# Moving the norm between two transformer blocks behind the first weights of the second block

## What is computed

```
def first_block(x, ...):
    h = x
    for l in range(DEPTH):
        ...
        h = h + 0.5 * swiglu_ffn(rms_norm(h, ffn2_norm[l]), ffn2_w_in[l], ffn2_w_out[l])
    return rms_norm(h, final_norm)

def second_block(x, ...):
    for l in range(DEPTH):
        x = x + 0.5 * swiglu(rmsnorm(x, norm_ffn1[l]), w_ffn1_in[l], w_ffn1_out[l])
        ...
    return rmsnorm(x, norm_final)
```

## Time and profile before

| | us |
|---|---|
| median of 3 runs | 2809.01 |
| lowest and highest | 2804.11, 2813.02 |
| the profiled execution: its own time | 2811.83 |
| its span from first to last instruction | 2809.9 |
| PE busy | 2701.6 (96% of the span) |
| DVE busy | 1546.6 (55%) |
| ACT busy | 1381.6 (49%) |
| POOL busy | 236.2 (8%) |

### The profile page before, as it was taken

One profiled execution on the slowest core, in us unless ns is written; L12 is line 12 of the kernel. 1 busy time (PEld: TensorE's weight loads), 2 busy tenths in 40 slices (PEclk: granted clock), 3 DMA queues, 4 the chain that ended last, 5 costly groups with the idle time before them and its releaser, 6 DMA issues.

```text
span 2809.9 us, 39469 instructions
## 1 busy us (share of the span) xinstructions
PE 2701.6 (96%) x14978; PEld 2312.9 (82%) x14978; DVE 1546.6 (55%) x2107; ACT 1381.6 (49%) x2168; POOL 236.2 (8%) x147
## 2 busy tenths in 40 slices
PE   8999899899999998989999999999999999999998
PEld 6879887788888898877887889888888888888887
DVE  5556735455555566455555556456555554556654
ACT  5447235454544452445544444455544444455543
POOL 0100201000000002100010000342000000243000
PEclk9999999999999999999999999999999999999999
DMA  6554213355555441244854554324555555323553
GB/s 246 187 172 155 69 48 118 111 176 186 180 187 187 136 142 39 83 129 129 220 188 159 184 187 155 109 98 150 180 187 181 186 187 166 120 94 125 195 186 136
DMA packets 117659, 426.48 MB, mean 152 GB/s; under 512 B 12988, under 2 KB 14780, under 8 KB 117116
## 3 DMA queue, kind: packets, MB, share of 16 engines
q1 hardware_dynamic: 117008, 423.55, 45.8%
q10 hardware_dynamic: 492, 0.68, 0.1%
HBM read 422.74 MB, written 1.44 MB: 151 GB/s over the span
## 4 chain that ended last, share of the span: by engine, by line
PE 89%; DVE 6%; ACT 3%; issue 1%; DMA 0%; POOL 0%; DVEq 0%; ACTq 0%
PE bank L433 73%; PE bank L453 3%; PE bank L1446 2%; DVE lo_slots L421 2%; PE bank L625 1%; PE bank L1493 1%; PE bank L1462 1%; ACT hi_slots L407 1%; PE bank L572 1%; PE bank L990 1%; PE bank L1001 0%; PE bank L782 0%; PE bank L771 0%; ACT xn L540 0%; PE bank L1476 0%
## 5 line engine op out<-in xcount | busy, mean ns | idle before, releaser
L421 DVE TENSOR_TENSOR lo_slots<-raw,hi_slots 128x1024 fp32r<-128x1024 f32 x740 | 914.8, 1241 | 797.0 <-ACT hi_slots L407 796.9
L407 ACT ACTIVATE hi_slots<-raw 128x1024 fp32r<-128x1024 f32 x788 | 830.8, 1057 | 690.7 <-PE bank L433 663.3
L433 PE MATMUL bank<-hi_slots,x_hi 128*128 128x512 f32 x1600 | 635.1, 397 | 14.3 <-DVE x_lo L604 8.9
L433 PE MATMUL bank<-hi_slots,x_lo 128*128 128x512 f32 x1600 | 625.4, 391 | 0.0
L433 PE MATMUL bank<-lo_slots,x_hi 128*128 128x512 f32 x1600 | 624.3, 390 | 0.0
L433 PE MATMUL bank<-x_hi,hi_slots 128*128 128x256 f32 x1280 | 376.3, 294 | 3.3 <-DVE x_lo L604 2.3
L433 PE MATMUL bank<-x_lo,hi_slots 128*128 128x256 f32 x1280 | 367.3, 287 | 0.0
L433 PE MATMUL bank<-x_hi,lo_slots 128*128 128x256 f32 x1280 | 366.6, 286 | 0.0
L433 PEld LDWEIGHTS bank<-hi_slots,x_hi 128*128 128x128 f32 x1600 | 301.9, 189 | 77.0 <-issue 13.2
L433 PEld LDWEIGHTS bank<-hi_slots,x_lo 128*128 128x128 f32 x1600 | 301.4, 188 | 64.3
L433 PEld LDWEIGHTS bank<-lo_slots,x_hi 128*128 128x128 f32 x1600 | 302.1, 189 | 59.5
(11 more groups left out here) (294 smaller groups left out, 2967.0 us busy)
## 6 DMA issues: line engine op xcount, KB each, us to landing
raw<-w_full SPq DMA_DIRECT2D x792, 512.0 KB, 3.3
bias_mem<-bias_rows SPq DMA_DIRECT2D x8, 288.0 KB, 6.9
const<-consts SPq DMA_DIRECT2D x1, 1664.0 KB, 7.1
h<-x_t SPq DMA_DIRECT2D x1, 1024.0 KB, 5.1
mem<-mem_t SPq DMA_DIRECT2D x1, 1024.0 KB, 10.2
final<-finals SPq DMA_DIRECT2D x2, 512.0 KB, 7.4
out_t<-h SPq DMA_DIRECT2D x4, 256.0 KB, 2.3
bias_rows<-final ACTq DMA_DIRECT2D x1, 384.0 KB
```

Source lines behind the costliest of these rows:

```text
L407: nc.scalar.activation(w_hi[s], raw[s][:, :], ACT.Copy).then_inc(hi_ready[s], 1)
L421: nc.vector.tensor_tensor(w_lo[s], raw[s][:, :], w_hi[s].bitcast(F32), ALU.subtract).then_inc(lo_ready[s], 1)
L433: mm = nc.tensor.matmul(out, lhsT=a, rhs=b, start=start and n == 0, stop=stop and n == len(passes) - 1)
```

## The change

The change gives the block seam the form of a layer seam. The first half of the unscaled `h` is transposed in the middle of the last down units and the second half after the first unit of the second block. The gain that goes with `x_hi` and `x_lo` is the product `seam_gain` of the first block's final gain and the second block's first gain, computed once at the program's start. The factor per token of the first norm is kept in `rstd_first`. `h` is still rescaled in place, now while PE works on the first up group; then the second norm's squares, mean, roots and reciprocals follow, and `rstd` becomes the product of both factors, which the first `Silu` waits for (`rstd_both`). These steps are placed between the first three splits of the new FFN. The parameters grow by 8 columns, from 440 to 448.

```diff
+        def dve_seam_state(E):
+            state = E.state(0)
+            dve.wait_ge(sems["rstd"], state * TT)
+            nc.vector.tensor_copy(rstd_first[:, :], rstd[:, :]).then_inc(sems["rstd_first"], 1)
+            dve.wait_ge(sems["final_loaded"], 16)
+            for hf in range(2):
+                two = slice(hf * HALF, (hf + 1) * HALF)
+                for t in range(TT):
+                    nc.vector.scalar_tensor_tensor(out=h[:, t, two], in0=h[:, t, two], scalar=rstd[:, t:t + 1],
+                                                   in1=final[:, two], op0=ALU.mult, op1=ALU.mult).then_inc(sems["h_ready"], 1)
+        def dve_seam_mean(E):
+            dve.wait_ge(sems["rstd_first"], 1)
+            dve_mean(E.state(0))
+        def dve_seam_rstd(E):
+            state = E.state(0)
+            for t in range(TT):
+                dve_rstd(state, t)
+            dve.wait_ge(sems["rstd"], (state + 1) * TT)
+            nc.vector.tensor_tensor(rstd[:, :], rstd[:, :], rstd_first[:, :], ALU.mult).then_inc(sems["rstd_both"], 1)
+            dve.wait_ge(sems["rstd_both"], 1)
...
+        def act_ffn(E, u0, n, state, late, opening=()):
             f = E.ffn(n)
             for i in range(3):
                 split_hi(E, u0 + i)
+                if i < len(opening):
+                    opening[i](E)
+            if opening:
+                act.wait_ge(sems["rstd_both"], 1)
...
-                    pe_ffn(E, 0, E.normed(0), 0, turn(E.state(0), 1, FFN_TURNS), nothing)
+                    pe_ffn(E, 0, E.normed(0), 0, turn(E.state(0) - seam, 1, FFN_TURNS), nothing)
...
-                    late = turn(E.state(n_last), 0, FFN_TURNS) if E.l < DEPTH - 1 else nothing
+                    late = turn(E.state(n_last), 0, FFN_TURNS) if E.block == 0 or E.l < DEPTH - 1 else nothing
...
+                    nc.vector.tensor_tensor(seam_gain[:, :], param[:, AT_FINAL:AT_REL],
+                                            param[:, AT_SECOND + SECOND_COLS["ffn1"][0]:AT_SECOND + SECOND_COLS["ffn1"][1]],
+                                            ALU.mult).then_inc(sems["seam_gain"], 1)
...
+                        now = gain(after, "ffn1", 0, KT) if E.l < DEPTH - 1 else seam_gain
...
                         dve_turned(normed, 1, FFN_TURNS, now)
                         for t in range(TT):
                             dve_rstd(state, t)
+                        if E.l == DEPTH - 1:
+                            E.block, E.l = 1, 0
+                            dve_seam_state(E)
+                            E.block, E.l = 0, DEPTH - 1
```

More of the change, by code:

```diff
@@ L255, in build @@
         rstd = sb("rstd", [P, TT])
+        rstd_first = sb("rstd_first", [P, TT])
+        seam_gain = sb("seam_gain", [P, KT])
         ffn_mem, mix1, cross, mix2 = ExitStack(), ExitStack(), ExitStack(), ExitStack()
@@ L1992, in _ @@
                 first = E.state(0)
-                act_turned(E.normed(0), 0, FFN_TURNS, gain(E, "ffn1", 0, KT))
                 if E.block == 0:
+                    act_turned(E.normed(0), 0, FFN_TURNS, gain(E, "ffn1", 0, KT))
                     for s in range(2):
                         first_hi(s)
[L1997 to L2000, removed]
+                    act_turned(E.normed(0), 1, FFN_TURNS, gain(E, "ffn1", 0, KT))
+                    for s in range(2, SLOTS):
+                        first_hi(s)
+                    for hf in range(2):
+                        for t in range(TT):
+                            act_square(first, hf, t)
                     for t in range(TT):
-                        act_square(first, hf, t)
-                for t in range(TT):
-                    act_root(first, t)
+                        act_root(first, t)
                 for E.l in range(DEPTH):
@@ L2008, in _ @@
                         nc.scalar.activation(ab_now_hi[:, :], p1(E, "ab", 0, KT * 8), ACT.Copy).then_inc(sems["ab_hi"], 1)
-                    act.wait_ge(sems["rstd"], (E.state(0) + 1) * TT)
-                    act_ffn(E, 0, 0, E.state(1), nothing)
+                    if E.block == 0 or E.l > 0:
+                        act.wait_ge(sems["rstd"], (E.state(0) + 1) * TT)
+                    act_ffn(E, 0, 0, E.state(1), nothing, (act_seam_squares, act_seam_root) if E.block == 1 and E.l == 0 else ())
                     act_full(E.state(1), E.normed(1), FFN_TURNS, gain(E, "mix", 0, KT))
@@ L2044, in _ @@
                         after.block, after.l = E.block, E.l + 1
-                        now = gain(after, "ffn1", 0, KT)
+                        now = gain(after, "ffn1", 0, KT) if E.l < DEPTH - 1 else seam_gain
+                        if E.l == DEPTH - 1:
+                            act.wait_ge(sems["seam_gain"], 1)
                         act_ffn(E, E.last(), 1, state, lambda: act_turned(normed, 0, FFN_TURNS, now))
@@ L2075, in _ @@
                 gain = (p1, p2)[E.block]
[L2076 to L2084, removed]
+                if E.block == 0:
+                    dve_turned(E.normed(0), 0, FFN_TURNS, gain(E, "ffn1", 0, KT))
+                    for s in range(2):
+                        first_lo(s)
+                    dve_turned(E.normed(0), 1, FFN_TURNS, gain(E, "ffn1", 0, KT))
+                    for s in range(2, SLOTS):
+                        first_lo(s)
+                    dve_mean(E.state(0))
+                    for t in range(TT):
+                        dve_rstd(E.state(0), t)
+                    nc.vector.tensor_tensor(seam_gain[:, :], param[:, AT_FINAL:AT_REL],
+                                            param[:, AT_SECOND + SECOND_COLS["ffn1"][0]:AT_SECOND + SECOND_COLS["ffn1"][1]],
+                                            ALU.mult).then_inc(sems["seam_gain"], 1)
                 for E.l in range(DEPTH):
@@ L2090, in _ @@
                                                 ALU.subtract).then_inc(sems["ab_lo"], 1)
-                    dve_ffn(E, 0, 0, 1, nothing)
+                    dve_ffn(E, 0, 0, 1, nothing, (dve_seam_mean, dve_seam_rstd) if E.block == 1 and E.l == 0 else ())
                     if E.block == 0 and E.l == 0:
```

26 lines of the change are left out of this document (19 added, 7 removed).

## The result

| | before | after |
|---|---|---|
| median, us | 2806.99 (5 runs) | 2791.10 (5 runs) |
| lowest and highest | 2802.35, 2813.02 | 2788.39, 2793.49 |
| the profiled execution: its own time, its span | 2811.83, 2809.9 | 2793.49, 2791.5 |

The ratio is 0.9943, 95% interval 0.9928 to 0.9958. The kernel gained 16 us, where 8.9 were forecast. The time lies 2 us under the range.

A forecast was written before the change was run, and what follows sets the result against it. PE, busy 96% of the span, was taken as the bound, with time to win only where it idles or clocks lower. Gain 9.20 - 0.3 - 0 = 8.9 us, from 2809.01 to 2800.1 us, range 2793 to 2808.

The forecast's parts named there:

- The seam: Block seam: its stretch becomes a layer seam's plus a small wait of PE; net gain 8.9 us.
- Gross 9.20: Block seam's 55.90 us less a layer seam's 46.70, from first half's addition to first hidden transposes.
- a stall of 0.3: PE waits 0.3 us for the first product `hid` after group 1's first unit; bounds 0 and 0.7.
- The stretch: From the first half's addition to the first hidden transposes at the block seam: 47.0 us, within 46.7 to 47.4.
- The chain behind it: Second norm's work on DVE and ACT beside the first up group; `hid` ready at 2170.9, PE wants it at 2170.62.
- The slot 0 remainder: On DVE at the block seam, ends some 10.5 us after the last down matmul's start, 1.6 us early for PE.
- the Trainium skill's figure: Table load ahead of the first Silu: a further drain of about 1.38 us; stall 1.7 us, gain 7.5 us.
- What else is added: `seam_gain` at the start is hidden; the parameters' load grows by 8 columns, counted 0, at most 0.1 us.
- More than 9.2: Rival: a larger gain, needing another place that the seam disturbs now; chance 0.04.
- Slower: Rival: late rescalings on DVE hold back unit 4 and all splits; 0.3% slower at 19 us late; chance 0.02.
- given back later: Rival: weights' stream is the real limit, PE waits later instead; time 2806 to 2809 us; chance 0.05.
- the bound of 0.3%: Whole kernel: least change told from none, 8.4 us, so faster means below 2800.6 us; chance of faster 0.51.

The follow-up runs named there:

- 32 bytes more: The changed kernel with an unused tile of 32 bytes per partition behind its new tiles; 2797.37 us, ratio 0.9963.
- the run with 32 bytes of padding ahead of `x_hi`: The kernel before with 32 unused bytes ahead of `x_hi` and 32 behind `x_lo`; 2828.64 us, ratio 1.0071.
- before + 32: The kernel before with one unused tile of 32 bytes per partition ahead of the FFN's tiles; 2807.62 us, ratio 0.9998.
- before + 64: The kernel before with an unused tile of 64 bytes per partition ahead of the FFN's tiles; 2806.69 us, ratio 0.9989.
- the last version: The changed kernel with 64 bytes of padding and the mixers' copy of `x` 192 bytes further on; 2779.04 us, ratio 0.9890.

## Why the prediction was wrong, step by step

**The seam: right.** Gross 9.20 less a stall of 0.3 was 8.9; it was 9.1. The stretch was forecast at 47.0 and is 46.07. Of the difference 0.71 is the faster down pitch, which isn't the seam's; 0.15 is the stall, which was 0.15 us instead of 0.3 (PE started on `hid` 0.38 us after the last matmul, where 0.23 is the pitch). With 32 bytes more, at the old pitch, the stretch is 46.68.

**The chain behind it: right within 0.3 us.** The slot 0 remainder ends at 1504.07 + 1.23 = 1505.30, 10.3 us after the last down matmul's start (forecast 10.5). The copy took 0.17 (I took 0.12). The first Silu starts 1.30 us after its table load, as in the earlier trace rows. By the Trainium skill's figure ("ScalarE: Activation LUTs", section "What ACT_TABLE_LOAD costs") another 1.38 us would lie there; this trace shows none of it either. The clock is 1.00, the eight early transposes are there, and no wait for `lo_slots` at group 1.

**"What else is added": the failed step.** The prediction costed the new tiles by the instructions that fill them and said "I count 0, at most 0.1". What they did was push `hid_hi` and `hid_lo` by 96 bytes, from distance 96 to 192 of the slots, and so take 5 ns off each of 2112 down matmuls. By the stretches that is a term of -10.7 us for the down phases; the up groups' +1.7 comes with it. Sum with both: 9.1 + 10.7 - 1.7 = 18.1 for 8.9, by the two profiles; by the medians it is 15.9. The rival that held it was "More than 9.2", which "would need another place that the seam disturbs now, for which I see no row", with a chance of 0.04. There was no row of before that could give its size; but the addresses of both programs could have been compared, and that all the FFN's buffers shift was to be seen there. The right use would have been a wider range, to both sides: the run with 32 bytes of padding ahead of `x_hi` shows that a shift can as well cost 20 us.

**The range.** That the time fell out of it has a share of chance. The forecast stands 9.0 us above the measured time; 7.0 are the gain that it lacked, and 2.0 are the median of before, which came out at 2806.99 with five runs where the prediction started from 2809.01 with three. From that start a gain of 15.9 would have given 2793.1, just inside the range; the gain itself was 1.8 times the forecast one either way.

**"Slower" and "given back later": both false.** PE lost none of the 9 us behind the seam.

**The chances.** The sum put the forecast half a us from the bound of 0.3%. With 9.1 us alone the ratio would be 0.9968, 0.7 us on the faster side of the bound of 0.9970; with 32 bytes more it was 0.9963, with an interval to 0.9976 that takes the bound in. That the result is clearly faster is owed to the addresses, which the prediction didn't have.

**Open:** why the up groups take 0.21 us more in the change (0.22 in before + 32, 0.07 in change + 32, 0 in before + 64), with `x` and slots unmoved, 0.4 ns on each matmul; why the three passes of one layout differ; and by what mechanism the distance acts. No run tells whether streaming the moving operand or loading the held one is what gets slower.

## What to carry to other kernels

A new tile isn't free because its instructions are: compare the addresses of the large matmul operands in both programs, and if any moved against another, measure the change with and without a pad that puts it back. When an experiment is to isolate a mechanism, keep the addresses modulo 256 as they were; otherwise it can be off by 10 to 20 us here for a reason that isn't its own. And once the best distance for each width of matmul is known (here 0 for 512 columns and 64 for 256), a few bytes of padding are worth more than the whole restructured seam: 9 us of the 30 that the last version won are the seam's.

## What the runs showed of the hardware

At the full clock, the distance from one 128x512 matmul with 4-byte operands to the next is 226.7 to 234.3 ns, and from one 128x256 to the next 113.9 to 120.0, by the difference of the held and the moving operand's addresses in their partitions modulo 256 bytes, with no other engine at work (three places of the moving operand at 512 columns, one at 256). At 128 columns it is 111.5 to 111.8 at every place of the held operand. A stretch of PE with 1.50 us of idle time in it kept the clock at 1.00, where 4.53 us brought it to 0.50.
